# Indexer of a hybrid attention block on one core: queries and scores for tokens from 256 on, a narrow key product, and two gate weights prepared on GpSimd

## The reference, cut to what matters

```
h = rms_norm(x) * (1 + scale) + shift                 # 1024 tokens x 1024 channels
qi, ki, wi, aa, ba, gates = h @ w_in                  # slices of one projection
wi = wi * (8 ** -0.5 * 64 ** -0.5)
dots  = einsum('qhd,sd->qhs', qi, ki)                 # 8 index heads of 64, one shared key row of 64
score = einsum('qh,qhs->qs', wi, relu(dots)); score = -inf where key > query
sel   = top_k(score, 256)                             # attention then sees only these keys
```

## Time and profile before

| | us |
|---|---|
| median of 3 runs | 1498.63 |
| the runs | 1492.21, 1499.35, 1498.63 |
| the profiled execution | 1497.45 |
| its span | 1495.7 |

### The profile page before, as it was taken

One profiled execution on the slowest core, in us unless ns is written; L12 is line 12 of the kernel. 1 busy time (PEld: TensorE's weight loads), 2 busy tenths in 40 slices (PEclk: granted clock), 3 DMA queues, 4 the chain that ended last, 5 costly groups with the idle time before them and its releaser, 6 DMA issues.

```text
span 1495.7 us, 26635 instructions
## 1 busy us (share of the span) xinstructions
PE 1444.0 (97%) x10144; PEld 894.5 (60%) x10152; DVE 947.8 (63%) x1972; ACT 716.4 (48%) x1508; POOL 562.8 (38%) x644
## 2 busy tenths in 40 slices
PE   7999899999998989999999999999999999999997
PEld 6454796444443566677676676655446777754444
DVE  3768877777532577677778776545725676747434
ACT  4546777776442535555555544333214666621111
POOL 0181477778772424522522512003002444456000
PEclk9999999999999999999999999999999999999999
DMA  9300044324324222322322322336562000065132
GB/s 373 104 1 29 17 119 120 123 96 137 101 77 137 59 72 58 87 59 58 86 59 58 87 55 71 103 99 244 176 234 97 30 16 30 16 221 186 44 113 85
DMA packets 137319, 147.20 MB, mean 98 GB/s; under 512 B 16642, under 2 KB 109418, under 8 KB 135532
## 3 DMA queue, kind: packets, MB, share of 16 engines
q1 hardware_dynamic: 136348, 141.05, 29.7%
q10 hardware_dynamic: 720, 4.46, 0.7%
q0 software_dynamic: 128, 0.03, 0.0%
HBM read 114.40 MB, written 31.15 MB: 97 GB/s over the span
## 4 chain that ended last, share of the span: by engine, by line
PE 60%; DVE 3%; ACT 2%; POOL 2%; issue 1%; DMA 0%; SPq 0%; DVEq 0%; POOLq 0%
PE ps L92 15%; PE ps L94 15%; PE ps L93 14%; PE ps L2306 2%; PE ps L1786 1%; PE ps L1838 1%; PE ps L1883 1%; DVE g_o L1647 1%; PE ps L1844 1%; PE ps L1850 1%; DVE g_yq L1512 1%; PE ps L1824 1%; PE ps L1904 1%; PE ps L1832 1%; PE ps L1888 1%
## 5 line engine op out<-in xcount | busy, mean ns | idle before, releaser
L92 PE MATMUL ps<-g_h_hi,g_piece_hi 128*128 128x512 f16 x544 | 207.8, 382 | 5.1 <-PEq L2498 5.1
L93 PE MATMUL ps<-g_h_lo,g_piece_hi 128*128 128x512 f16 x544 | 207.4, 381 | 0.0
L94 PE MATMUL ps<-g_h_hi,g_piece_lo 128*128 128x512 f16 x544 | 207.4, 381 | 0.0
L1282 POOL TENSOR_TENSOR g_shared<-g_shared 128x120 f32<-128x120 f32 (+14 forms) x120 | 57.7, 481 | 206.8 <-DMA g_shared<-diagonal_blocks 196.2
L932 DVE TENSOR_SCALAR_CACHE_REDUCE a_ada<-a_ada,a_s_all 128x896 bf16<-128x896 f32 (+1 forms) x124 | 113.1, 969 | 1.0
L2452 POOL TENSOR_SCALAR g_o<-g_o,l_share 128x128 f32<-128x128 f32 (+3 forms) x64 | 47.7, 745 | 152.3 <-DVE l_share L2412 152.1
L92 PE MATMUL ps<-g_o,g_h_hi 128*128 128x128 f16 (+2 forms) x424 | 101.4, 266 | 1.0 <-DVE l_b L2427 1.0
L94 PE MATMUL ps<-g_o,g_h_lo 128*128 128x128 f16 (+2 forms) x424 | 101.4, 266 | 0.4
L93 PE MATMUL ps<-g_o,g_h_hi 128*128 128x128 f16 (+2 forms) x416 | 98.3, 264 | 0.0
L1512 DVE SCALAR_TENSOR_TENSOR g_yq<-e_raw,g_taps,g_yq 128x1024 f32<-128x1024 f32 x60 | 84.9, 1414 | 15.9 <-ACT g_yq L1346 14.1
L94 PEld LDWEIGHTS ps<-g_h_hi,g_piece_lo 128*128 128x128 bf16 x544 | 53.5, 98 | 65.1 <-issue 1.7
(11 more groups left out here) (430 smaller groups left out, 4255.6 us busy)
## 6 DMA issues: line engine op xcount, KB each, us to landing
a_w<-in_w_in SPq DMA_DIRECT2D x17, 1024.0 KB, 5.6
g_piece<-in_w_in SPq DMA_DIRECT2D x34, 512.0 KB, 3.8
channel_gates<-a_ada SPq DMA_DIRECT2D x48, 256.0 KB, 2.2
g_shared<-diagonal_blocks SPq DMA_DIRECT2D x32, 256.0 KB
a_ada<-in_w_ada ACTq DMA_DIRECT2D x4, 1024.0 KB, 9.3
a_x<-in_x SPq DMA_DIRECT2D x8, 512.0 KB, 9.3
delta_gate<-a_ada SPq DMA_DIRECT2D x16, 256.0 KB, 2.5
g_shared<-sums_by_head SPq DMA_DIRECT2D x8, 512.0 KB, 4.3
```

The source lines that it names most:

```text
L92: pe.matmul(out, a_hi, b_hi, start=first, stop=False)
L93: pe.matmul(out, a_hi, b_lo, start=False, stop=False)
L94: return pe.matmul(out, a_lo, b_hi, start=False, stop=last)
L1282: nc.gpsimd.tensor_tensor(part, table[:, j, :, j + 1:BASE], tc[:, :, j:j + 1].broadcast_to([P, NT, left]), ALU.mult).then_inc(sub, 1)
```

## The change

- Units exist for tiles 2 to 7 only: 48 instead of 64, in 40 items, an item being one unit or the pair (3, e) with (2, e + 1) or (3, e + 1) with (2, e), whose matmuls are issued in turn. Four items are in flight. ACT's Relu of tiles 6 and 7 is split in two parts, each started by its own semaphore step.
- Dots are products of 64 rows: even heads use rows 0 to 63 and odd heads rows 64 to 127 of queries and keys. The keys are written once (rows 0 to 63) and copied to rows 64 to 127 by four SBUF-to-SBUF DMAs on SP.
- Queries of the first half are made for tokens 256 to 511 only. The first four transposes of the second half stand before block m = 2, the last four among its matmuls; `low_q(3)` moves behind `low(10)` on DVE.
- The key product has 88 output rows: 64 key rows and the 24 small ones, which ACT copies out and PE turns with 8 small transposes.
- The memsets of `k_hi`, `k_lo` go. `constants`, the bias rows and the y / neg steps change place on DVE.
- GpSimd casts the weights of gate unit 1 itself, right behind those of unit 0; ACT no longer does.
- `constants` now waits for the key product's second half (`k_mm` 2) before it writes.
- For tiles 0 and 1 the mask comes from the causal table instead of score rows.

```diff
-NS = 152
+NS = 88
-        units = [(i, e) for pair in ((7, 0), (6, 1), (5, 2), (4, 3)) for e in range(8) for i in pair]
+        items = []
+        for e in range(0, IDX_HEADS, 2):
+            items += [((3, e), (2, e + 1))] + [((i, e),) for i in (7, 6, 5, 4)] + [((i, e + 1),) for i in (7, 6, 5, 4)] + [((3, e + 1), (2, e))]
+        units = [unit for item in items for unit in item]
...
         def _(sp):
...
+            for half in range(HALVES):
+                cols = slice(half * BANK, (half + 1) * BANK)
+                sp.wait_ge(kh_ok, half + 1)
+                sp.dma_start(k_hi[64:128, cols], k_hi[0:64, cols]).then_inc((twin_low, twin_high)[half], 16)
+                sp.wait_ge(kl_ok, half + 1)
+                sp.dma_start(k_lo[64:128, cols], k_lo[0:64, cols]).then_inc((twin_low, twin_high)[half], 16)
             sp.wait_ge(rows_ok, 2)
...
         def _(pool):
...
-            nc.gpsimd.memset(k_hi, 0.0)
-            nc.gpsimd.memset(k_lo, 0.0).then_inc(zero, 1)
-            nc.gpsimd.tensor_copy(pair(s_hi), s32[:, :, 0:64].unsqueeze(2).broadcast_to(twice))
-            nc.gpsimd.tensor_copy(s_hi[:, :, P:NS], s32[:, :, 64:88]).then_inc(s_cast, 1)
+            nc.gpsimd.tensor_copy(s_hi, s32).then_inc(s_cast, 1)
...
             def high(v, x, of):
-                if v == 0:
+                if v < 2:
...
             weights(0)
+            weights(1)
             for u in range(UNITS):
-                if u + 1 < UNITS:
+                if 0 < u < UNITS - 1:
                     weights(u + 1)
...
         def _(pe):
...
             def query(m, half, k):
-                cols = slice(half * BANK, (half + 1) * BANK)
+                cols = slice(NEAR, BANK) if half == 0 else slice(BANK, T)
...
             for m in (1, 2, 3):
+                if m == 2:
+                    for n in range(4):
+                        turn(KD + n)
                 pe.wait_ge(q_ready, m + 1)
...
-                    if m > 1 and k % 2:
-                        turn(KD + 4 * (m - 2) + k // 2)
+                    if m == 2 and k % 2:
+                        turn(KD + 4 + k // 2)
...
-                    last = three(nc.tensor, bank(4 + half), s_hi[:, k, 0:P], s_lo[:, k, 0:P],
+                    last = three(nc.tensor, bank(4 + half)[0:NS], s_hi[:, k], s_lo[:, k],
...
-            for i in range(NT):
-                for k in range(KD):
-                    last = three(nc.tensor, g.ps[:, 6 * BANK + i * 24:6 * BANK + (i + 1) * 24], ...)
+            def turn_small(half):
+                pe.wait_ge(small_t_ok, half + 1)
+                pe.wait_ge(ql_ok, 3)
+                for i in range(4 * half, 4 * half + 4):
+                    last = nc.tensor.transpose(g.ps[:, 6 * BANK + i * 24:6 * BANK + (i + 1) * 24], small_t[:, i * P:(i + 1) * P], ...)
+                last.then_inc(small_mm, 1)
+            def index(k):
+                if k == 0:
+                    pe.wait_ge(ql_ok, 6)
+                    pe.wait_ge(twin_low, 32)
+                elif k == 1:
+                    pe.wait_ge(ql_ok, 8)
+                    pe.wait_ge(kl_ok, 2)
+                elif k == 2:
+                    pe.wait_ge(kl_ok, 2)
+                    pe.wait_ge(small_t_ok, 2)
+                elif k == 3:
+                    pe.wait_ge(small_ok, 1)
+                    pe.wait_ge(rows_ok, 1)
+                elif k == 5:
+                    pe.wait_ge(twin_high, 32)
+                if k >= 4:
+                    pe.wait_ge(acc, done_by[k - 4])
+                def products(i, e):
+                    rows, tok = slice(64 * (e % 2), 64 * (e % 2) + 64), slice(i * P, (i + 1) * P)
+                    for c0, c1 in ((c0, min((i + 1) * P, c0 + BANK)) for c0 in range(0, (i + 1) * P, BANK)):
+                        at = k % 4 * T + c0 + BANK * (i == 2)
+                        for step, (a, b) in enumerate(((q_hi, k_hi), (q_hi, k_lo), (q_lo, k_hi))):
+                            last = nc.tensor.matmul(g.ps[:, at:at + c1 - c0], a[rows, e // 2, tok], b[rows, c0:c1], start=step == 0, stop=step == 2)
...
+                for _ in itertools.zip_longest(*(products(i, e) for i, e in items[k])):
+                    pass
+            turn_small(0)
+            index(0)
+            turn_small(1)
+            for k in range(1, len(items)):
+                index(k)
...
         def _(act):
...
                 act.wait_ge(k_mm, half + 1)
-                nc.scalar.copy(k_hi[0:64, 0, cols], bank(4 + half)[0:64])
-                nc.scalar.copy(k_hi[64:128, 1, cols], bank(4 + half)[64:128]).then_inc(kh_ok, 1)
+                if half:
+                    nc.scalar.copy(small_t[:, cols], bank(4 + half)[64:88]).then_inc(small_t_ok, 1)
+                nc.scalar.copy(k_hi[0:64, cols], bank(4 + half)[0:64]).then_inc(kh_ok, 1)
+                if half == 0:
+                    nc.scalar.copy(small_t[:, cols], bank(4 + half)[64:88]).then_inc(small_t_ok, 1)
...
             for n, (i, e) in enumerate(units):
-                act.wait_ge(dots, n + 1)
-                nc.scalar.activation(relu[:, n % 4, 0:(i + 1) * P], relu[:, n % 4, 0:(i + 1) * P], ACT.Relu).then_inc(relu_ok, 1)
+                for part, (c0, c1) in enumerate(parts_of(i)):
+                    act.wait_ge(dots, parts_by[n] - len(parts_of(i)) + part + 1)
+                    nc.scalar.activation(dots_at(n)[:, c0:c1], dots_at(n)[:, c0:c1], ACT.Relu).then_inc(relu_ok, 1)
             def high(v, x, of):
-                if v < UNITS:
+                if 2 <= v < UNITS:
...
         def _(dve):
...
+            for half in range(HALVES):
+                dve.wait_ge(kh_ok, half + 1)
+                nc.vector.tensor_tensor(k_lo[0:64, cols], bank(4 + half)[0:64], k_hi[0:64, cols], ALU.subtract).then_inc(kl_ok, 1)
+                if half == 0:
+                    dve.wait_ge(rows_mm, 1)
+                    nc.vector.tensor_copy(bias_rows[:, 0], g.ps[0:H, 7 * BANK:7 * BANK + K_BUCKETS]).then_inc(rows_ok, 1)
+                    dve.wait_ge(rows_ok, 1)
+                    nc.vector.tensor_scalar(bias_rows[:, 1], bias_rows[:, 0], bias_rows[:, 0, 0:1], None, ALU.subtract).then_inc(rows_ok, 1)
+            constants()
+            dve.wait_ge(small_ok, 1)
+            nc.vector.tensor_scalar(small[:, :, 0:8], small[:, :, 0:8], H ** -0.5 * IDX_DIM ** -0.5, None, ALU.mult).then_inc(small_ok, 1)
...
             for u in range(UNITS):
                 if u == 0:
                     dve.wait_ge(t_low, 2)
-                    constants()
                     begin()
+                    dve.wait_ge(load, 48)
+                    nc.vector.tensor_tensor(y[:], small[:, :, 8:16], dt[:].unsqueeze(1).broadcast_to(everywhere), ALU.add).then_inc(step_v, 1)
+                    dve.wait_ge(step_v, 1)
+                    nc.vector.tensor_scalar(neg[:], y[:], 0.0, None, ALU.max).then_inc(step_v, 1)
...
                 if u == 13:
+                    nc.vector.memset(spent_of(1)[:, 0:P], 0.0)
                     for i in range(2):
-                        nc.vector.tensor_scalar(spent_of(i), rows_of(i), BELOW * 0.9, CLOSED, ALU.is_le, ALU.mult)
+                        nc.vector.tensor_scalar(spent_of(i)[:, i * P:(i + 1) * P], late[:, K_CAUSAL - K_KEPT:K_CAUSAL - K_KEPT + P], BELOW * 0.9, CLOSED, ALU.is_le, ALU.mult)
```

More of the change, by code:

```diff
@@ L15 @@
 from contextlib import ExitStack
+import itertools
 import numpy as np
@@ L31 @@
 IDX_DIM = 64
+IDX_HEADS = 8
 RANK = 256
@@ L433, in _ @@
-            last.then_inc(small_mm, 1)
-            pe.wait_ge(ql_ok, 4)
-            pe.wait_ge(rel_in, 32)
-            nc.tensor.matmul(g.ps[0:H, 7 * BANK:7 * BANK + K_BUCKETS], rel[:], onehot[:], start=True, stop=True).then_inc(rows_mm, 1)
-            for n, (i, e) in enumerate(units):
-                if n == 0:
-                    pe.wait_ge(ql_ok, 8)
-                    pe.wait_ge(kl_ok, 4)
-                elif n == 2:
-                    pe.wait_ge(kl_ok, 4)
-                elif n == 3:
+                if half == 0:
+                    pe.wait_ge(ql_ok, 4)
+                    pe.wait_ge(rel_in, 32)
+                    nc.tensor.matmul(g.ps[0:H, 7 * BANK:7 * BANK + K_BUCKETS], rel[:], onehot[:], start=True, stop=True).then_inc(rows_mm, 1)
@@ L455, in _ @@
-                last.then_inc(dots, 1)
+                elif k == 5:
[8 more added lines that the diff above has]
+                            last = nc.tensor.matmul(g.ps[:, at:at + c1 - c0], a[rows, e // 2, tok], b[rows, c0:c1], start=step == 0, stop=step == 2)
+                            if step == 2 and (i >= 6 or c1 == (i + 1) * P):
+                                last.then_inc(dots, 1)
+                            yield
@@ L821, in _ @@
             low_q(2)
-            low_q(3)
             for n in range(KD, 2 * KD + 1):
@@ L827, in _ @@
                     low(n - 1)
+                if n == KD + 3:
+                    low_q(3)
             nc.vector.memset(g.eps[:], EPS)
@@ L888, in _ @@
-            dve.wait_ge(acc, len(units))
```

(1 more changed line is left out.)

126 lines of the change are left out of this document (51 added, 75 removed).

## The result

The changed kernel takes 1478.89 us (median of four runs, 1473.70 to 1481.53), the one before 1498.70 us in the same comparison (four runs, 1492.21 to 1499.35): ratio 0.9881, 95% interval [0.9842, 0.9921]. It is faster, by about what was forecast (1478; range 1468 to 1487). The ratio is the recorded estimate over all these runs and stands for 17.8 us (11.8 to 23.7 by the interval); the two medians alone lie 19.8 us apart. The profiled execution of the changed kernel took 1477.58 us, span 1475.7, against a span of 1495.7 before: 20.0 us.

The account below looks back on a forecast made before the run. PE's stream plus its waits bound the kernel, the index stage going from a PSUM slot round trip to DVE. Gate units 19.7 us earlier, including the 6.1 and 9.2 gains: 1497.45 - 19.7 = 1477.8, said as 1478, range 1468 to 1487.

Parts of the forecast that it names:

- Queries: First-half query blocks 1 to 3 with 256 instead of 512 columns: the key product starts 6.1 us earlier.
- Keys and small projections: Key product and small transposes up to DVE's first score: it comes at 96.6 instead of 105.76, 9.2 us earlier.
- The index stage: Score loop paced by DVE, 43.0 us without idle time instead of 53.5; last score at 139.6.
- Rival A: Score loop falls back to a PSUM slot round trip, 9 us of DVE idle time: 1487; chance 12%.
- Row tiling: About seven changes of rows in use on PE, nearly all before the dots: nothing, at most 0.7 us.
- rival D: Weight loads of half-height matmuls are not hidden: gate units from 158.6, total 1497; chance 5%.
- Gate weights 1: Casts moved from ACT to GpSimd, ready at 122: worth 0; rescaling may shrink from 7.74 to 3.2 us.
- rival C: Unit 1's hole closes or leaves the clock at 2.4 GHz: 1.8 to 4.8 us more, 1473 to 1476; chance 12%.
- the clock loss there: Slower PE clock behind unit 1's 3.03 us hole, 1.8 us, said to move unchanged with the rest: 0.
- the gate units start at 139.7: End of the score loop: gate units start at 139.7 instead of 159.4, 19.7 us earlier in all.
- covered, by little: PE's index dots, 42.2 us plus 0.6 from 94.3, counted as hidden behind DVE, nearly as long.
- Rival E: PE does not hold 2.4 GHz on half of the rows: slower, 1510 to 1518; chance 4%.

Follow-up runs that it names:

- full_queries: The changed kernel with the first half's queries made for all 512 tokens again: 1479.55 us, ratio to before 0.9909.
- small_by_product: The changed kernel with 192 small matmuls again in place of the eight small transposes: 1476.86 us, ratio to before 0.9886.
- mixed_in_turn_off: The changed kernel with the two units of a mixed item issued one after the other, not in turn: 1475.91 us, ratio to before 0.9886.
- changed_once_more: The changed kernel measured again with no edit: 1476.59 us (six runs, 1471.55 to 1482.82), ratio to before 0.9883.
- steps_ahead_of_unit0: unit0_ahead_of_the_loops_end plus ACT's step-size chain moved ahead of unit 0's first copy, its DVE operations ahead of the score loop: 1475.49 us, ratio to before 0.9885.
- steps_ahead_full_height: steps_ahead_of_unit0 with dots over all 128 rows (scores are other numbers): 1471.62 us (five runs), ratio to before 0.9844.
- unit0_ahead_of_the_loops_end: The changed kernel with PE starting gate unit 0 at the score loop's fourth last item, not after the whole loop: 1472.07 us, ratio to before 0.9843.
- weights1_on_act: The changed kernel with the seven casts of gate weights 1 back on ACT in unit 0: 1478.39 us, ratio to before 0.9880.
- full_height_dots: The changed kernel with index-loop dots over all 128 rows (scores are other numbers), item 1 waiting for the key copy: 1478.30 us, ratio to before 0.9881.

## Why the prediction was right

Point by point:

- **Queries**, "6.1 us earlier": right. 7.0 in the first trace, 4.9 to 7.0 over all kernels with the narrow queries (the late ones have 3.4 us at half clock near 28, some of them near 47 too); undone, 6.25 come back. PE idled 1.62 us around block 2 (forecast 1.7), and DVE stayed in time.
- **Keys and small projections**: (7,0) on PE at 93.54 (forecast 94.3), first score at 95.69 (96.6), 10.1 us earlier instead of 9.2; constants and scaling took 2.37 us, forecast 2.4. The cast of 128 columns took 0.96 beside GpSimd, 0.23 before in unit 0; the same cast right behind it took 0.21, so the cost falls on some operations and not on others.
- **The index stage**, 43.0: it took 42.07, near the low bound, since all units ran at about the rate of the best pair. (The bound was given as 41.9; its own terms give 42.2 with the 0.6 for first units and 41.6 without.) No idle time. Rival A, 9 us of round trips, did not happen, with Relu in two parts or in one.
- **Row tiling** and **rival D**: 18 matmuls of up to 512 columns on 64 rows took 3.56 us from 93.54, 0.198 each on average, and those of 512 columns follow each other 0.216 apart (105.14, 105.35): their loads are hidden. D is out. (Its sum was 1.2 too high besides: 94.3 and 63.1 are 157.4, not 158.6.) The transposes, 0.42 for four, started 0.07 us before the dots ahead of them ended: no cost of a changed tiling shows.
- **Gate weights 1**: 0, right (0.2 at most); rescaling 3.29 (forecast 3.2). The 3.03 us of idle time in unit 1 moved unchanged, so the first half of rival C, that the hole closes, is out. Its second half, that the clock stays up behind the hole, did not come in the changed kernel's two profiles, but did in three variants with the same hole (full_queries, small_by_product, mixed_in_turn_off). The prediction took the clock loss there as a fixed term; it is one that some executions have.
- **The step that was off**, though the sum hides it: "the gate units start at 139.7" with nothing lost behind. They started at 137.78, 1.9 us better, but I had counted PE as "covered, by little", and did not ask what PE does once it is through its dots: it idled 2.89 us, 1.87 before, and this time the clock fell behind it, in unit 0, where PE is the bound. That cost 1.5 us. 21.6 - 1.5 = 20.1 stands beside the forecast 19.7. The sum is exact because two errors offset each other, and the median because of the runs that it was taken from: that is luck. In changed_once_more the medians lie 17.3 us apart (1493.88 and 1476.59).
- **Rival E**, 4%: the mechanism occurs, in part. It was priced for the whole loop, 1510 to 1518; what comes is 7 to 17 us at half clock in the profiles of four variants, which costs 2.0 to 5.2 us of the loop (44.08, 45.46, 46.13 and 47.32 us for 42.07). That is far from its turning point of half the dots: the 17 us hold 60 of the 240 matmuls, and DVE absorbs part. "Each slow stretch I read follows an idle one" was read from a trace in which no loop of half-height work existed.

What is shown and what is not: the changed kernel and its variants on 64 rows have 13 of 54 runs at a mean clock of 0.987 or under, the two variants on 128 rows none of 11, the kernel before none of 41. The pair steps_ahead_of_unit0 and steps_ahead_full_height, whose kernels differ in the height and the wait that it needs alone, is the strongest: four of six against none of five. If height made no difference, a split as one-sided as this would come by chance about once in 22 cases, and none of 11 against 13 of 54 about once in 15 (estimates from the counts). So that the height of the matmuls is what lets these stretches last is a conjecture that the runs favour, and it is not shown. Three things stand against more. The two kernels of the pair ran on different chips. No execution at 0.987 or under was profiled, and the four profiles with a long stretch in the loop lie at 0.988 to 0.991, so the counts do not say where the low runs lost their clock. And full height also ends the side-by-side work, which keeps PE busy for more of the loop: 23.00 of 23.00 us in the last row of steps_ahead_full_height, 20.68 in the changed kernel. Not tried: both heights in turn on one chip with every execution profiled, and keeping 64 rows while filling the gaps ahead of the loop.

The best kernel that computes the reference's scores is unit0_ahead_of_the_loops_end: 0.9843 [0.9820, 0.9865], against 0.9883 [0.9856, 0.9910] for the changed kernel. The intervals overlap by little; the trace has 4.5 us of it. By its stages steps_ahead_of_unit0 is 2.1 us better still, which its six runs, four of them at low clocks, do not show.

## What to carry to other kernels

When one stage is shortened, look at the engine that now finishes early: its wait for the stage's end can cost twice, once as idle time and again as half clock in the work behind it, and a wait for just the part that is needed removed both here (4.5 us for three lines). A stage that leaves PE half of its rows should be priced with a clock that may stay at 1.2 GHz for a part of it, as it did in four of eleven profiles here, and run where another engine sets the pace. An edit that is to take an overlap away has to be seen to do so in the trace before its time is read. And where the clock moves totals by more than a part is worth, judge the part by the starts of stages, not by the median.

## What the runs showed of the hardware

- On 64-row matmuls, PE busy without a gap, the granted clock stayed at 0.50 for 6.8 to 17.1 us in four of eleven profiles and at 1.00 in seven. The Trainium skill, "TensorE: Matmul & The Clock Gate", Part 1, ties the clock to how busy PE has been recently. Here PE's busy share was 1.00 throughout such stretches, so by the profile's busy time alone they can't be foreseen.
- Two products on different 64-row halves do run side by side: six matmuls in 0.82 us, 1.31 one after the other at full height. They do so whether the two are issued in turn or one behind the other (0.82 us in mixed_in_turn_off as well).
- Small operations of DVE can pay for a working GpSimd, and accumulation out of PSUM does not. An addition and a maximum of 64 columns took 0.66 and 0.50 us ahead of the loop in steps_ahead_of_unit0, 0.23 and 0.20 in unit 0 of the changed kernel; six rescalings 3.29 without GpSimd, 6.90 with it (weights1_on_act). Not each one pays: of two equal casts in a row one took 0.96 and the next 0.21. The 42 accumulations took 36.13 us without idle time, with GpSimd at work for the first half.
- The idle time of 2.89 us ahead of unit 0 came with half clock (3.4 or 6.8 us, from within it or just behind it) in both profiles of the changed kernel and in five of the six other kernels that kept the wait; idle times of 1.87 us before the change and 1.96 in full_height_dots did not. No length separates the cases: 2.00 us ahead of (7,0) came with half clock in steps_ahead_full_height and without it in full_height_dots, and the 3.03 us in unit 1 came with it in seven of ten profiles.
